# A two-layer trunk on eight cores: new cost figures in the planner that orders five engine queues, and one RMSNorm's squares summed on VectorE

## The reference, cut to what matters

```python
def reference(x, c, ...):
    for layer in range(2):
        sh1, sc1, g1, sh2, sc2, g2 = ada_modulation(c, ada_w[layer], ada_b[layer])
        h = rmsnorm(x, norm_mix_g[layer]) * (1.0 + sc1) + sh1
        if layer == 0:      # gated short convolution beside a gated linear recurrence
            p = h @ w_in0
            y = concat(short_conv_mixer(...), hgrn2_mixer(...)) @ w_out0
        else:               # spatial gating: u * (W_s layernorm(v) + b) in chunks of 128
            y = spatial_gating_mixer(gelu(h @ w_in1 + b_in1), ...) @ w_out1
        x = x + g1 * y
        h = rmsnorm(x, norm_ffn_g[layer]) * (1.0 + sc2) + sh2
        x = x + g2 * (square(relu(h @ w_ff1[layer])) @ w_ff2[layer])
    return rmsnorm(x, final_g)
```

## Time and profile before

| | us |
|---|---|
| median of 3 runs (slowest core) | 2879.95 (2876.72 to 2883.79) |
| profiled execution | 2877.11 |
| its span on the slowest core, core 5 | 2875.6 |
| spans of the other cores | 2845.4 to 2873.3 |
| PE busy / DVE busy / ACT busy, core 5 | 2748.3 / 1393.5 / 1276.9 |
| mean granted TensorE clock, core 5 | 0.984 of full speed |

### The profile page before, as it was taken

The page is one execution under the profiler, slowest core; times in us unless marked ns, Lnnn a source line. Parts: engine busy times, 40 slices in busy tenths (PEclk is TensorE's granted clock), DMA queues, the critical chain, the costliest instruction groups (busy, mean ns, idle before and its releaser), DMA issues.

```text
span 2875.6 us, 40978 instructions; the slowest of 8 cores (2845.4 to 2875.6 us)
## 1 busy us (share of the span) xinstructions
PE 2748.3 (96%) x14271; PEld 1270.3 (44%) x14271; DVE 1393.5 (48%) x2567; ACT 1276.9 (44%) x2023; POOL 80.1 (3%) x99
## 2 busy tenths in 40 slices
PE   3989999989999999999998999998999999999998
PEld 1444444444444444444444444443444444444443
DVE  1778888784323323233232776763435335345343
ACT  3767777783313313223232776743324324224232
POOL 1000000000000000000000000000000000000000
PEclk7999999999999999999999999999999999999999
DMA  9864444389614034043058566669011011011000
GB/s 179 148 148 126 130 131 132 118 158 177 124 26 88 27 62 88 8 81 81 4 118 162 166 196 189 180 174 198 1 59 59 1 59 59 1 59 59 1 30 30
DMA packets 174603, 275.88 MB, mean 96 GB/s; under 512 B 11456, under 2 KB 84928, under 8 KB 174400
## 3 DMA queue, kind: packets, MB, share of 16 engines
q1 hardware_dynamic: 89936, 198.81, 22.0%
q0 software_dynamic: 84464, 74.45, 18.4%
HBM read 280.56 MB, written 67.11 MB: 121 GB/s over the span
## 4 chain that ended last, share of the span: by engine, by line
PE 84%; DMA 7%; DVE 3%; issue 3%; ACT 3%; SPq 0%; DVEq 0%; ACTq 0%; POOLq 0%
PE ps L429 84%; DMA sb_arena<-ada_w 3%; DMA sb_arena<-xs 3%; ACT sb_arena L433 2%; DVE sb_arena L442 1%; DVE sb_arena L439 1%; DMA xs<-sb_arena 1%; ACT sb_arena L435 1%; DMA sb_arena<-w_in 1%; ACT L339 0%; SPq L453 0%; PE ps L725 0%; DVE sb_arena L693 0%; DVE sb_arena L1121 0%; DVEq L337 0%
## 5 line engine op out<-in xcount | busy, mean ns | idle before, releaser
L429 PE MATMUL ps<-sb_arena 128*128 128x512 bf16 (+3 forms) x13185 | 2691.1, 366 | 42.5 <-ACT sb_arena L433 9.3
L429 PEld LDWEIGHTS ps<-sb_arena 128*128 128x128 bf16 (+1 forms) x13185 | 1222.2, 98 | 1478.7 <-issue 91.7
L439 DVE TENSOR_TENSOR sb_arena<-sb_arena 128x512 bf16<-128x512 bf16 (+3 forms) x1224 | 659.3, 550 | 799.5 <-ACT sb_arena L433 743.9
L433 ACT ACTIVATE sb_arena<-ps 128x512 bf16<-128x512 f32 (+2 forms) x705 | 413.3, 597 | 1122.4 <-PE ps L429 1076.6
L442 DVE SCALAR_TENSOR_TENSOR sb_arena<-ps,sb_modc,sb_arena 128x512 f32<-128x512 f32 x384 | 287.4, 749 | 507.3 <-PE ps L429 457.9
L433 ACT ACTIVATE sb_arena<-sb_arena 128x512 f32<-128x512 f32 (+4 forms) x720 | 383.2, 564 | 252.8 <-DVE sb_arena L442 87.5
L435 ACT ACTIVATE sb_arena<-sb_arena,sb_modc,sb_s1c 128x512 bf16<-128x512 f32 x256 | 201.6, 812 | 122.0 <-DVE sb_arena L439 101.3
L339 ACT ACT_TABLE_LOAD x116 | 148.8, 1283 | 2.0
L439 DVE TENSOR_TENSOR sb_arena<-ps,sb_arena 128x512 f32<-128x512 f32 (+1 forms) x128 | 87.3, 684 | 26.9 <-PE ps L429 26.0
L442 DVE SCALAR_TENSOR_TENSOR sb_arena<-sb_arena,sb_vcol 128x512 f32<-128x512 f32 x128 | 90.9, 747 | 14.1 <-ACT sb_arena L433 10.9
L442 DVE SCALAR_TENSOR_TENSOR sb_arena<-sb_arena,ps 128x128 f32<-128x128 f32 x256 | 87.3, 342 | 18.5 <-PE ps L429 11.5
(11 more groups left out here) (39 smaller groups left out, 222.0 us busy)
## 6 DMA issues: line engine op xcount, KB each, us to landing
sb_arena<-xs SPq DMA_DIRECT2D x192, 256.0 KB, 5.1
sb_arena<-x SPq DMA_DIRECT2D x160, 256.0 KB, 4.6
xs<-sb_arena SPq DMA_DIRECT2D x128, 256.0 KB, 5.1
sb_arena<-xs SPq DMA_DIRECT2D x64, 512.0 KB, 6.2
sb_arena<-w_ff POOLq DMA_DIRECT2D x32, 1024.0 KB, 20.4
sb_arena<-ada_w POOLq DMA_DIRECT2D x48, 512.0 KB, 8.2
xs<-sb_arena SPq DMA_DIRECT2D x32, 512.0 KB, 3.1
out<-sb_arena SPq DMA_DIRECT2D x32, 512.0 KB, 2.7
```

What stands on the lines that cost most here:

```text
L429: return e.matmul(out, lhsT, rhs, start=start, stop=stop, skip_group_check=skip)
L433: f = lambda e: e.activation(out=out, in_=in_, func=func, scale=scale)
L439: return P.op(q, lambda e: e.tensor_tensor(out=out, in0=in0, in1=in1, op=op), reads, writes, cost)
```

## The change

The planner's figures are replaced: costs of several operations; how long an engine's result takes to be seen by another, for each pair (`SEEN`, with 0.3 us of slack towards PE); 5.0 us (POOL) and 4.0 us (SP) from a DMA's last byte to its landing in place of 2.0; a short overlap of neighbours on ACT and DVE (`TAIL`). A PE operation may now take banks only if enough stay free for the oldest PE operation that still has to take some. In m1 `n1a` sums squares with `sum_sq` and one matmul; `pre` prepares tile 1, then tile 0, each from four loads of two chunks, with squares put into `h` and eight matmuls; `run` doesn't prepare tile 1 any more. `h1` moves to slot 9, and the slots of ffn1's weights change with it.

```diff
-    SEM_LAT = 0.12
+    SLACK = 0.3
+    TAIL = {"pe": 0.0, "act": 0.09, "dve": 0.085, "pool": 0.0, "sp": 0.0}
+    SEEN = {("pe", "pe"): 0.0, ("pe", "act"): 0.15, ("pe", "dve"): 0.11, ("act", "act"): 0.17, ("dve", "dve"): 0.17,
+            ("act", "dve"): 0.1, ("dve", "act"): 0.1, ("act", "pe"): 0.145 + SLACK, ("dve", "pe"): 0.145 + SLACK}
+    SEM_LAT = 0.15
+    LANDS = {"pool": 5.0, "sp": 4.0}
...
+        takers = sorted((o.i for o in ops if o.take), key=lambda i: -ops[i].key)
...
+                while takers and ops[takers[-1]].end is not None:
+                    takers.pop()
...
-                if q == "pe" and len(ops[i].take) > nfree:
-                    continue
+                if q == "pe" and len(ops[i].take) > nfree - (len(ops[takers[-1]].take) if takers and takers[-1] != i else 0):
+                    if ops[i].take:
+                        continue
...
-                end = dma_free[q] + 2.0
+                end = dma_free[q] + self.LANDS[q]
...
-                free[q] = end
+                free[q] = end - min(self.TAIL[q], 0.5 * o.cost)
...
-                        lat = 0.0 if (po.q == x.q and x.q == "pe") else self.SEM_LAT
+                        lat = 0.1 if po.dsem is not None else self.SEEN.get((po.q, x.q), self.SEM_LAT)
...
-                P.op("pe", f, [b, b_sil], [bank[bk]], 0.55)
+                P.op("pe", f, [b, b_sil], [bank[bk]], 0.379)
...
+                mq, mqb = sq_bufs(R.o, "m1q")
...
-                h1, hb1 = R.take("m1h1", [128, 8, TT], BF16, 8)
+                h1, hb1 = Region(9 * SLOT).take("m1h1", [128, 8, TT], BF16, 8)
...
                 def n1a(t):
-                    nbk[t] = norm_a(t, xs_d, xb, xr, xrb, sq, sqb)
+                    for c in range(8):
+                        s = x_load((xr, xrb, 0), xs_d, xb(t, c), c, t)
+                        sum_sq(xr[:, s, :], xrb[s], c, mq, mqb)
+                    bk = nbk[t] = next_main()
+                    P.op("pe", lambda e: mm(e, ps[:, bk, :], onesD[:], mq[3], True, True), [b_small, mqb[3]], [bank[bk]], 0.216)
...
                 def pre():
                     P.key_shift = -300
-                    n1a(0)
-                    n1i(0)
-                    n1b(0)
+                    for t in (1, 0):
+                        h, hb = hs[t], hbs[t]
+                        for q in range(4):
+                            dma("sp", xr[:, 2 * q:2 * q + 2, :], xs_d[t, :, 2 * q:2 * q + 2, :],
+                                xsb[t][2 * q:2 * q + 2], xrb[2 * q:2 * q + 2], xls[q], 1 << 19)
+                        for c in range(8):
+                            act(h[:, c, :], xr[:, c, :], AF.Square, [xrb[c]], [hb[c]])
+                        bk = next_main()
+                        group8(bk, lambda k: onesD[:], lambda k: h[:, k, :], [b_small] + hb)
+                        norm_inv(bk, invB, b_inv)
+                        for c in range(8):
+                            tb = c % 2
+                            tt(tmp[:, tb, :], xr[:, c, :], invB, ALU.mult, [xrb[c], b_inv], [tmpb[tb]])
+                            act(h[:, c, :], tmp[:, tb, :], AF.Identity, [tmpb[tb], b_mod[1][0], b_s1[1][0]], [hb[c]], 0.8,
+                                bias=mod(1, 0, c), scale=scol(1, 0, c))
...
-                    n1a(1)
                     v_rs()
-                    n1i(1)
                     v_ln()
-                    n1b(1)
...
-            f1 = ffn(1, True, [2, 7, 8, 9, 6, 0, 12, 13], [10, 11, 4, 5, 15, 1, 3, 14])
+            f1 = ffn(1, True, [2, 7, 8, 10, 6, 0, 12, 13], [11, 4, 5, 9, 15, 1, 3, 14])
```

More of the change, by code:

```diff
@@ L137, in op @@
                 if x.w is not None:
-                    assert b.w is not None and x.w < b.w, (b.name, x.name)
+                    assert b.w is not None and x.w <= b.w, (b.name, x.name)
                     preds.add(x.w)
@@ L429, in mm, with act @@
                 return e.matmul(out, lhsT, rhs, start=start, stop=stop, skip_group_check=skip)
-            def act(out, in_, func, reads, writes, cost=0.6, table=None, bias=None, scale=1.0):
+            def act(out, in_, func, reads, writes, cost=0.61, table=None, bias=None, scale=1.0):
                 if bias is None:
@@ L627, in norm_a, with sq_bufs, sum_sq @@
                 return bk
+            def sq_bufs(off, name):
+                a, ab = Region(off).take(name, [128, 3, TT], F32, 3)
+                b, bb = Region(off + 6144).take(name + "b", [128, TT], BF16)
+                return [a[:, 0, :], a[:, 1, :], a[:, 2, :], b], ab + bb
+            def sum_sq(x, xb, c, q, qb):
+                if c == 0:
+                    act(q[2], x, AF.Square, [xb], [qb[2]])
+                    return
+                i = c % 2
+                act(q[i], x, AF.Square, [xb], [qb[i]])
+                o = 3 if c == 7 else 2
+                tt(q[o], q[i], q[2], ALU.add, [qb[i], qb[2]], [qb[o]])
             def norm_inv(bk, invB, b_inv):
@@ L727, in fT @@
                     return ins
-                P.op("pe", fT, [Kb[u], b_small], [bank[BT]], 0.4)
+                P.op("pe", fT, [Kb[u], b_small], [bank[BT]], 0.223)
                 act(kdT[:, u, :], psT[:, 0:512], AF.Copy, [bank[BT]], [kdTb[u]])
@@ L755, in fU @@
                     return ins
-                P.op("pe", fU, [kdTb[u]] + vb, [bank[BU[0]], bank[BU[1]]], 0.8)
+                P.op("pe", fU, [kdTb[u]] + vb, [bank[BU[0]], bank[BU[1]]], 0.36)
                 BO = next_main()
@@ L765, in fI @@
                     return ins
-                P.op("pe", fI, [scTb[u]] + vb, [bank[BO]], 0.4)
+                P.op("pe", fI, [scTb[u]] + vb, [bank[BO]], 0.223)
                 act(Sb[:, u * 8, :], Sc[:, j, :], AF.Copy, [Scb[j]], [Sbb[u * 8]], 0.28)
@@ L969, in norm_f @@
                     bk = next_main()
-                    P.op("pe", lambda e: mm(e, ps[:, bk, :], onesD[:], hq[3], True, True), [b_small, hqb[3]], [bank[bk]], 0.25)
+                    P.op("pe", lambda e: mm(e, ps[:, bk, :], onesD[:], hq[3], True, True), [b_small, hqb[3]], [bank[bk]], 0.216)
                     act(inv, ps[:, bk, :], AF.Ln, [bank[bk], b_small], [invb_], 0.7, T_EXP, epsc[:, 0:1])
@@ L1017, in final_norm @@
                     bk = next_main()
-                    P.op("pe", lambda e: mm(e, ps[:, bk, :], onesD[:], fq[3], True, True), [b_small, fqb[3]], [bank[bk]], 0.25)
+                    P.op("pe", lambda e: mm(e, ps[:, bk, :], onesD[:], fq[3], True, True), [b_small, fqb[3]], [bank[bk]], 0.216)
                     act(fiv, ps[:, bk, :], AF.Ln, [bank[bk], b_small], [fivb], 0.7, T_EXP, epsc[:, 0:1])
@@ L1078, in m1 @@
                 R = Region(88 * KB, 120 * KB)
-                sq, sqb = R.take("m1sq", [128, 8, TT], BF16, 8)
+                mq, mqb = sq_bufs(R.o, "m1q")
+                R.o += 8 * KB
                 vn, vnb = R.take("vn", [128, 4, D], BF16, 4)
@@ L1157, in f @@
                         return ins
-                    P.op("pe", f, vnb + [wmb], [bank[bk]], 0.4)
+                    P.op("pe", f, vnb + [wmb], [bank[bk]], 0.223)
                     r = ec % 2
```

37 lines of the change are left out of this document (13 added, 24 removed).

## The result

The changed kernel takes 2844.45 us (median of 3 runs, 2842.31 to 2848.33), 0.9878 of before, 95% interval 0.9852 to 0.9904: faster by 35.5. Forecast: 2844.0. Its profiled execution took 2844.45, with a span of 2842.6 on core 2. (Some executions have a die at a lower granted clock and take longer; ratios leave them out, and where too few others were left, profiled executions or single cores are compared and named.)

The account below looks back on a forecast made before the run. PE was taken to bound the kernel, busy 2748.3 of 2875.6 us. The terms sum to -36.0 against the profiled 2877.1, giving 2841; with 2.8 for the median of the runs, 2844, range 2824 to 2868.

Parts of the forecast that it names:

- beginning: First mixer, 72 to 216 us: longer filler before a piece and more room after results, -6, bounds 0 and -12.
- steady m0: 216 to 576 us: more room in PE's list after DVE and ACT results, -2, bounds +4 and -4.
- m0 to ffn0: 576 to 720 us: no wait seen to be removed, 0, bounds -9 and +9.
- modulation pieces in ffn0: Longer fillers ahead of the pieces' loads cut PE's waits of 7.7: -5.9, bounds 0 and -7.7.
- ffn0 to m1: Tile 1 first and earlier loads remove the waits around tile 0's norm: -11, bounds -4 and -15.9.
- matmuls and adds: In m1, 42 fewer norm matmuls, -9.1; DVE's adds in their place, +2, bounds 0 and 28.9.
- m1 to ffn1: One bank emptied earlier and one ACT table change fewer shorten PE's waits: -4, bounds +2 and -15.
- ffn1: After 2016 us: same work in the same order of stages, left as it is.
- Rival C: In m1 a late load now stops DVE as well as ACT: slower, 2890 us; chance 0.05.
- Rival A: New order wins nothing on the chip; only the matmuls and about 6 of ffn0 to m1: 2865 us; chance 0.13.
- Rival B: All stage changes become clean, idle time and low clock both go: 31 less, 2813 us; chance 0.10.

Follow-up runs that it names:

- E5: Changed kernel with the old norm in m1's tiles 2 to 7: eight bf16 squares and eight norm matmuls, no DVE adds; 0.9903 of before.
- E10: New m1 code with the old planner and costs, only the landing figures new (5.0 and 4.0); 0.9931 of before.
- E3: Changed kernel with the landing figures put back to 2.0 on both queues; 0.9942 of before.
- E6: Changed kernel with only tile 0 normalised ahead of m1, tile 1's norm back inside m1; span of the profiled execution 2845.5 us, no ratio.
- E13: E8's kernel with the planner's slack of 0.3 set to 0.0; 0.9955 of before.
- E8: Changed kernel with eight instead of four buffers in the ring of m1's residual loads; 0.9836 of before.
- E18: Changed kernel with residual loads of chunks 4 to 7 using the norm's four buffers in each mixer's last two tiles, not the last alone; 0.9847 of before.
- E2: New m1 code with the old planner figures, bank rule and costs; 0.9913 of before.
- E1: Changed kernel with the old m1 code put back, keeping the new planner and durations; 0.9939 of before.

## Why the prediction was right, and where it was not

By the table's starts the span between PE's first and last marks fell by 33.6 on the slowest core; the sum had 36.0. The last column has the difference of the medians of the eight cores.

| step | predicted | measured, slowest core | median of the cores |
|---|---|---|---|
| to ffn0: beginning, steady m0, m0 to ffn0 | -6 - 2 + 0 = -8 | -3.2 | -7.2 |
| modulation pieces in ffn0 | -5.9 | -8.9 | -7.6 |
| ffn0 to m1 | -11 | -15.0 | -12.6 |
| m1's tiles: matmuls and adds | -9.1 + 2 = -7.1 | -11.0 | -7.7 |
| m1 to ffn1 | -4 | +4.3 | +3.5 |
| ffn1 | 0 | +0.2 | +1.4 |

The mechanisms of the large terms held. That the sum came within 3 us is luck in part: on the slowest core three steps gave more than I took and two less. One of the two, *to ffn0*, comes near the forecast in the median of the cores; the other, m1 to ffn1, goes the wrong way in both columns.

*Matmuls and adds.* E5 measures 7.5 for the 7.6 of five norms, so the +2 for adds was too much. The sixth norm, 1.5, lies in the row above. The rest of the 11.0 is waits: PE no longer waits in m1's tiles, and the 2.7 idle of the earlier trace rows, which the slowest core had, is gone as well. A tile takes 43.4 (260.5 over six). Rival C has nothing behind it.

*Pieces.* All waits of the earlier trace rows went, not 5.9 of 7.7, and E10 and E3 show that the landing figure did it. I took a piece as 1 MB, but the profile pages of both kernels have 512 KB. For that the fit of the Trainium skill (DMA: Bandwidth & Descriptors, Anatomy of one DMA) gives about 3.2 us, an estimate, still further from the 10.78 measured.

*ffn0 to m1.* I wrote that the wait just goes and may come back by a few us; it went with all its low clock, 13.5 of the bound of 15.9 without tile 2's 1.5. E6 shows that the eight buffers did it, not tile 1's turn.

*Beginning and m0.* The beginning gained (idle 14.3 to 8.4; 11.8 to 15.2 on the eight cores before, 7.0 to 8.9 now). Half of 3.1 and as much again is 3.1 and not my 3.3, which leaves the -6 as it is. My reason, that 0.445 counted from a result gives PE more room, is only half of it: E13 shows that without the slack 28 are lost up to ffn0 (805.8 against E8's 778.0), E10 and E3 that the landing figures and the others must come together.

*The step that failed* is m1 to ffn1. "One bank is now emptied ahead of that add" looked at one add of the earlier trace rows, as if the wait hung on it. But it hangs on the late loads, and it moved. In both lists DVE has two residual evictions ahead of `ym4` to `ym7`. Before, DVE had stood 10.57 by then, and their loads had landed:

```profile
1939.98 1.40 DVE L442 SCALAR_TENSOR_TENSOR sb_arena<-ps,sb_modc,sb_arena 128x512 f32<-128x512 f32 x2
```

Now it comes to them at 1901.3, and stands 6.84 and 1.80. By that the wait of 4.22 and 5.34 became 12.50 and 7.01. I had costed the ring's loads as standing "in the same order" and not asked how old they are when DVE reaches them; the answer, outside my bound of +2, is shown by E8 and E18, where these evictions wait for no load and *to ffn1* falls to 37.0 and 36.7, and by E10 against E2, which puts the loss down to the landing figures.

At m0 to ffn0 the same mechanism stands in the profile of the slowest core. From tile 6's first output group to ffn0 the five kernels with the same lists take 44.3, 37.8 (E1), 45.8 (E5), 41.2 (E6) and 40.8 (E8), against 38.3 before: almost 4 more on the mean, within my bounds. How late the loads come differs from run to run and from core to core: the idle time from 576 to 720 is 10.1 to 17.7 on the changed kernel's cores, 8.9 to 11.1 before.

Rival A did not hold: the lists alone win 17.6 (E1). Rival B's clean changes came at one of three.

## What to carry to other kernels

A planner's figure is worth what stands around it: the landing times without the other new figures, and the others without them, each made m0 slower here, and a landing of 10 for all of SP's transfers to mend a few late ones cost 62 us against the changed kernel. Mend a late load where it is issued (more buffers, or ones that have become free), not in the figure. And when a list changes, ask of each eviction that moves up how long its load has been on the way.

## What the runs showed of the hardware

*A 256 KB transfer can take some three times its median.* From 1880 to 1915 of the changed kernel, core 2, beside five 1 MB weight loads (issues: count, KB each, median us to landing):

```profile
sb_arena<-w_ff POOLq DMA_DIRECT2D x5, 1024.0 KB, 30.1
xs<-sb_arena SPq DMA_DIRECT2D x6, 256.0 KB, 14.9
sb_arena<-xs SPq DMA_DIRECT2D x5, 256.0 KB, 12.8
```

The profile page has 4.6 and 4.9 for stores and loads of the whole program. On core 3, beside six such weight loads, they take 9.1 and 8.7, so the weight loads alone do not set it; the cause is not shown. The Trainium skill (DMA: Bandwidth & Descriptors, Anatomy of one DMA) fits about 2.0 us and the bytes over 436 GB/s to a DMA of the path that POOL's queue takes. That is about 4.4 us, an estimate, for 1 MB; the trace has 30.1 here as a median, and decides.

*The two cores of a pair differ.* Of cores 0 and 1, 2 and 3, 4 and 5, 6 and 7, one has a span some 20 to 27 us longer than the other, before and after, and not always the same one. Core 3 in the same execution, at the rows where core 2 waits 8.83 and 12.50:

```profile
627.12 0.59 PE L440 MATMUL ps<-sb_arena,sb_onesD 128*128 128x512 bf16 x1 [2.58 <-DVE sb_arena L450]
...
1892.29 15.66 PE L440 MATMUL ps<-sb_arena 128*128 128x512 bf16 x64 [3.58 <-DVE sb_arena L450]
```

There its 256 KB loads take 8.7 as a median from 1875 to 1915. With earlier loads (E18) the difference is 11 to 15. The Trainium skill (Trainium Architecture — The Big Picture, The hierarchy (trn2)) lists these pairs as sharing one HBM stack; that fits, and no run here isolates it.

*The clock falls behind a long wait.* After the waits of 12.50 and 7.01 the stretches 1915 to 1925, 1925 to 1940, 1940 to 1960 and 1960 to 1990 have 0.83, 0.85, 0.94 and 1.00 of the full 2.4 GHz: part of the first three was at 1.2 GHz.
